# Two orders changed on ScalarE of a one-core transformer layer: four early weight halves, and the transfers that spread the bias rows

## What is computed

```python
# first block
h = rmsnorm(x, norm_mix)
proj = h @ w_in                      # queries, keys, values of two attentions, gates
y_a = swa_sink_attention(...)        # 8 heads, window of 128 keys, bias by distance, one sink
y_b = nsa_attention(...)             # 8 heads: compressed keys, selected blocks, window; bias by distance
merged = sigmoid(g_a) * (y_a @ w_up_a) + sigmoid(g_b) * (y_b @ w_up_b)
x = x + merged @ w_out
ug = causal_dwconv(rmsnorm(x, norm_ffn) @ w_ffn_in, conv_w, conv_b)
x = x + (silu(g) * u) @ w_ffn_out
x = rmsnorm(x, norm_final)
# second block: latent, differential and memory attention, gate, output product
```

## Time and profile before

| what | value |
|---|---|
| median of 3 runs | 1166.47 us (1166.33 to 1166.97) |
| the profiled execution | 1168.41 us, of which the span of the core 1166.6 us |
| PE busy | 1082.8 us, 93% of the span |
| DVE / ACT / POOL busy | 54% / 50% / 33% |
| mean granted clock of PE | 0.962 of full speed |
| DMA | 109.24 MB, mean 94 GB/s |

### The profile page before, as it was taken

How to read it: one execution, slowest core, us unless ns; L and a number is a source line. 1 busy time by engine, 2 the same in 40 slices (tenths; PEclk the granted TensorE clock), 3 DMA queues, 4 the chain that set the end, 5 groups by cost and what they waited for, 6 DMA issues and landing times.

```text
span 1166.6 us, 15532 instructions
## 1 busy us (share of the span) xinstructions
PE 1082.8 (93%) x5162; PEld 894.9 (77%) x5162; DVE 626.5 (54%) x1431; ACT 582.3 (50%) x1176; POOL 389.8 (33%) x172
## 2 busy tenths in 40 slices
PE   6899899799999999999999999999899697888898
PEld 4779688689888787888888888888787576666677
DVE  4535544988835466454554453214255586477631
ACT  5443556888834244444444443324334263778841
POOL 1334544000014444344444444434443243200013
PEclk8989899899999999999999999999899899888999
DMA  5353343101103332223222233323233122341022
GB/s 191 84 165 129 108 138 101 42 19 47 44 34 130 117 101 89 90 94 104 90 99 99 90 107 129 107 90 108 95 130 118 54 91 91 86 113 37 2 72 108
DMA packets 38387, 109.24 MB, mean 94 GB/s; under 512 B 6795, under 2 KB 8971, under 8 KB 37643
## 3 DMA queue, kind: packets, MB, share of 16 engines
q1 hardware_dynamic: 27804, 89.70, 23.5%
q10 hardware_dynamic: 10528, 18.83, 5.1%
HBM read 99.99 MB, written 7.70 MB: 92 GB/s over the span
## 4 chain that ended last, share of the span: by engine, by line
issue 64%; POOL 16%; PE 10%; DVE 5%; ACT 3%; DMA 1%; POOLq 1%; ACTq 0%
POOL WLO L596 16%; PE PS L1680 2%; PE PS L1682 2%; PE PS L1681 2%; ACT PB L789 2%; DVE PB L1227 1%; PE PS L1875 1%; DMA X<-xT 1%; PE PS L1852 1%; DVE PB L1260 1%; POOLq L592 0%; PE PS L2031 0%; DVE PB L1262 0%; ACT HF L764 0%; DVE BLO L1142 0%
## 5 line engine op out<-in xcount | busy, mean ns | idle before, releaser
L596 POOL TENSOR_TENSOR WLO<-RAW,WHI 128x1024 fp32r<-128x1024 f32 x160 | 387.5, 2422 | 765.4 <-ACT WHI L610 765.2
L610 ACT ACTIVATE WHI<-RAW 128x1024 fp32r<-128x1024 f32 x162 | 171.2, 1058 | 318.3 <-PE PS L1682 305.3
L1680 PE MATMUL PS<-HHI,WHI 128*128 128x512 f32 x648 | 259.6, 401 | 28.7 <-POOL WLO L596 19.7
L1681 PE MATMUL PS<-HLO,WHI 128*128 128x512 f32 x648 | 256.7, 396 | 0.0
L1682 PE MATMUL PS<-HHI,WLO 128*128 128x512 f32 x648 | 256.4, 396 | 0.0
L1680 PEld LDWEIGHTS PS<-HHI,WHI 128*128 128x128 f32 x648 | 124.5, 192 | 60.1 <-issue 21.5
L1680 PE MATMUL PS<-BHI,WHI 128*128 128x512 f32 x368 | 146.1, 397 | 2.4 <-DVE BLO L1142 1.3
L1682 PEld LDWEIGHTS PS<-HHI,WLO 128*128 128x128 f32 x648 | 124.3, 192 | 26.5
L1681 PEld LDWEIGHTS PS<-HLO,WHI 128*128 128x128 f32 x648 | 124.3, 192 | 25.9 <-issue 0.5
L1682 PE MATMUL PS<-BHI,WLO 128*128 128x512 f32 x368 | 144.1, 391 | 0.0
L1681 PE MATMUL PS<-BLO,WHI 128*128 128x512 f32 x368 | 144.0, 391 | 0.0
(11 more groups left out here) (286 smaller groups left out, 1652.7 us busy)
## 6 DMA issues: line engine op xcount, KB each, us to landing
RAW<-wstream SPq DMA_DIRECT2D x162, 512.0 KB, 3.3
X<-xT ACTq DMA_DIRECT2D x4, 512.0 KB, 9.5
bias_b<-bias_rows ACTq DMA_DIRECT2D x2, 1024.0 KB
FX<-bias_b ACTq DMA_DIRECT2D x8, 256.0 KB, 2.7
X<-xT ACTq DMA_DIRECT2D x8, 256.0 KB, 3.6
x_keep<-X ACTq DMA_DIRECT2D x2, 1024.0 KB, 4.6
X<-x_keep ACTq DMA_DIRECT2D x2, 1024.0 KB, 5.0
outT<-X ACTq DMA_DIRECT2D x8, 256.0 KB, 2.5
```

What stands on the lines that cost most here:

```text
L596: pool.tensor_tensor(WLO[:, s, :], RAW[:, s, :], WHI[:, s, :].bitcast(F), ALU.subtract).then_inc(split_lo, 1)
L610: act.activation(WHI[:, c % 2, :], RAW[:, c % 2, :], ACT.Copy).then_inc(split_hi, 1)
L1680: pe.matmul(dst, a[0], b[0], start=first, stop=False, **kw)
L1681: pe.matmul(dst, a[0], b[1], start=False, stop=False, **kw)
```

## The change

ACT's list is reordered at four places, and the spreading of the bias rows is cut and moved.

- Projection loop: iteration 0 begins with `stream(4)`; iteration 1 has none; from iteration 2 on each begins with `stream(c + 3)`, one unit further ahead than before. The last one, in iteration 12, is `stream(15)`, so the vtok loop begins at its second unit.
- `stream(19)` moves from behind `blocks_high(1)` to ahead of it.
- `stream(59)` moves from behind the root of the norm to ahead of it.
- `bias_a` goes out in four DMAs of 2 heads (iterations 3 to 6), `bias_b` in four of 2 heads (iterations 7 to 10), `bias_c` in iterations 11 and 12. The wait before the attention is for all 16 DMAs.

```diff
             u = UNIT["proj"]
             for c in range(13):
-                if c >= 2:
-                    stream(u + c + 2)
+                if c != 1:
+                    stream(u + (c + 3 if c else 4))
                 if c < 11:
                     act.wait_ge(scaled, c + 1)
                     ps = PS[:, c % 4, :]
...
                 if c == 3:
                     act.wait_ge(st_rows, 16)
-                    act.dma_start(bias_a, bias_spread(0, 0, 256)).then_inc(spread, 16)
-                if c in (5, 7):
-                    half = (c - 5) // 2 * 4
-                    act.dma_start(bias_b[half:half + 4], bias_spread(8 + half, OH_A, SEQ, 4)).then_inc(spread, 16)
-                if c in (9, 10):
-                    for pg in range(4 * (c - 9), 4 * (c - 9) + 4):
+                if 3 <= c < 7:
+                    h = 2 * (c - 3)
+                    act.dma_start(bias_a[h:h + 2], bias_spread(h, 0, 256, 2)).then_inc(spread, 16)
+                if 7 <= c < 11:
+                    h = 2 * (c - 7)
+                    act.dma_start(bias_b[h:h + 2], bias_spread(8 + h, OH_A, SEQ, 2)).then_inc(spread, 16)
+                if c >= 11:
+                    for pg in range(4 * (c - 11), 4 * (c - 11) + 4):
                         src = bass.AP(tb_dram.tensor, 8 * OH + OH_A + OH_B + 15 * CMP_A + 9 - pg,
                                       [[OH, NH], [-CMP_A, 16], [1, CMP_W]])
                         act.dma_start(bias_c[:, 16 * pg:16 * pg + 16, :], src).then_inc(spread, 16)
...
-            for c in range(4):
+            for c in range(1, 4):
                 if c == 2:
                     blocks_high(0)
                 stream(u + c + 2)
...
             ins.then_inc(v_hi, 1)
+            stream(UNIT["gc"] + 2)
             blocks_high(1)
...
             u = UNIT["gc"]
             for c in range(len(AHEAD)):
-                stream(u + c + 2)
+                if c:
+                    stream(u + c + 2)
                 if c == 0:
-                    act.wait_ge(spread, 16 * 11)
+                    act.wait_ge(spread, 16 * 16)
                     bias_load(0)
                     bias_load(1)
...
             with act.Fori(1, 4) as i:
                 stream_and_norm("wout", 1, 1, x1_done, i)
+            stream(UNIT["ffn"] + 2)
             norm_root(2, RSTD)
...
                     for e in range(2):
                         c = u + 2 * s + e
-                        stream(c + 2, 4, i)
+                        if not isinstance(i, int) or s or e:
+                            stream(c + 2, 4, i)
```

## The result

The kernel became slower: a median of 1173.03 us (1172.98 to 1175.47, 4 runs) beside 1166.40 us of the kernel before on the same chip (1164.72 to 1166.97, 4 runs), a ratio of 1.0072 with a 95% interval of 1.0050 to 1.0094. The forecast was 1164.3 us. The profiled execution took 1175.47 us.

A forecast was written before the change was run, and what follows sets the result against it. PE was taken as the bound, busy 1082.8 of 1166.6 us. Unit 20 later (+0.35), clock recovery (+2.3) and unit 59 (-4.8) sum to -2.15, so 1166.47 became 1164.3 us; range 1158 to 1184.

The forecast's parts named there:

- What bounds the kernel: Whole kernel: PE busy 1082.8 of 1166.6 us, 23.4 us of its waits for `WLO`, with ACT late rather than POOL.
- Unit 4: Projection loop: its high part, no longer behind two evacuations, is ready ahead of PE, saving 3.57 us.
- unit 7: Projection loop: `bias_a` in quarters frees this unit's weight load, saving 3.01 us of stop and 3.0 of slow clock.
- Unit 19: High part ahead of `blocks_high(1)`: saves 2.9 us, or 1.5 with a slow rest, and 2.5 if the clock holds.
- The four terms together, unit 20 at 123.8: Savings of 3.57, 6.0, 2.9 and 2.5 us bring PE to unit 20 at 123.8 instead of 138.76.
- Two heads, two engines, one part after another: Bias transfers: each two-head DMA runs on the same two engines, in turn, at share about 0.13 and 51 GB/s.
- The sum of 83.8 us: Two engines' work on bias rows and weight loads from about 49.4; `spread` complete at 133.2, unit 20 at 139.1.
- This holds whatever the order, since the two engines never run dry: Bias transfers: `spread` completes at 133.2, or 133.5 with its landing, in whatever order the two engines' work comes.
- Unit 59: High part ahead of the norm's root: the 2.88 us stop and 1.9 of slow clock go, -4.8 us.
- ACT's queue takes no more: Rival, chance 0.15: issue blocks at some 175 unmoved rows per engine; unit 20 4.7 us late, about 1169 us.
- The rival of slow 1 KB rows: `bias_a` rows stay slow on two engines: 1196 us at 106 ns a row, 1177 at 70; chance 0.22.
- The rival of other engines: Bias parts find other engines or run side by side, `spread` complete by 118: 1146.8 us; chance 0.10.

The follow-up runs named there:

- proj_only: The kernel before with only the projection loop's and vtok loop's streams one unit further ahead, spreading as before: 1163.82 us, ratio 0.9986.
- spread4_only: The kernel before, its order of high parts kept, with the bias spreading in parts of 4 heads x 64 rows: 1161.95 us, ratio 0.9968.
- u19_only: The kernel before with only unit 19's high part moved ahead of `blocks_high(1)`: 1162.20 us, ratio 0.9970.
- heads4: The changed kernel with each bias part of 4 heads x 64 rows instead of 2 heads x 128 rows: 1146.11 us, ratio 0.9845.
- order_only: The changed kernel with the bias DMAs of the kernel before, the new order of high parts kept: 1153.28 us, ratio 0.9895.
- heads8: The changed kernel with bias parts of 8 heads x 32 rows instead of 2 heads x 128 rows: 1148.56 us, ratio 0.9857.
- spaced2: The spaced run with the short rows issued directly ahead of the wait for `spread` instead of behind unit 18: 1166.17 us, ratio 1.0011.
- ffn_only: The kernel before with only unit 59's high part moved ahead of the root: 1157.36 us, ratio 0.9938.
- narrow_b: The changed kernel with `bias_b` rows of 1 KB instead of 2 KB, second half of each row left out: 1156.62 us, one run.
- spread_only: The kernel before with only the bias DMAs of the changed kernel, its order of high parts kept: 1188.24 us, ratio 1.0200.
- spaced: The changed kernel with two-head `bias_b` parts in iterations 7, 9, 11 and behind unit 16, short rows behind unit 18: 1168.05 us, ratio 1.0029.

## Why the prediction was wrong, step by step

- **What bounds the kernel; that ACT is late and not POOL**: right. Each high part that came early took its stop away.
- **Unit 4, unit 7**: right in the mechanism. Both stops are gone in after, and none of its loads there took longer than 5.9 us, where unit 7's had taken 12.4. In the traces the sizes, 3.6 and 6.0, come out too: the matmul at 83.9 us of before runs at 74.9 in after, 9.0 earlier. In the times of the runs the edits gave less when each was made alone: 1.6 in `proj_only`, 3.7 in `spread4_only`.
- **Unit 19**: right in the stop, 2.21 in after, in `u19_only` and nearly so (2.23) in `heads4`, where 2.3 was said. The 2.5 us of clock beside it came whole in `order_only`, `heads4` and `heads8`, where unit 19 takes 5.6 us (7.97 before), and only in part elsewhere: it takes 7.18 in `u19_only` (128.25 to 135.43) and 7.19 in after.
- **The four terms together, unit 20 at 123.8**: right, once no long hold stood in the way: 122.81 in `heads4`, 126.08 in `heads8`. That `heads4` is nearer owes something to chance, as the two differ already ahead of these edits.
- **Two heads, two engines, one part after another**: right, and the main point of the forecast's argument. Share 0.13 and 51 GB/s, as it said; `bias_a` in by about 80 us, where it said 79. The sum of 83.8 us came out in `spaced2` (133.0). In after the last row had moved by 127.8: while PE stood, fewer loads of weights passed through the two engines, ten where the sum has 14.
- **"This holds whatever the order, since the two engines never run dry"**: this is the step that failed. It is true of the transfers and false of ACT. The sum took an issue as costing ACT some half a microsecond, however many rows lay ahead of it, so it let the high parts of units 13 to 18 go by undisturbed and had only the wait for `spread` stop PE. In after ACT was held in five places for 38.6 us, and PE stopped for 5.63, 4.96, 8.46 and 2.21 us ahead of unit 20, with the clock at a mean of 0.76 between 95 and 153 us where it is 1.00 in `heads4`. That put unit 20 at 152.59, with no wait at `spread` at all; in the forecast it was 139.1, and in `spaced2`, where only one hold stopped PE and the wait for `spread` covered it, 138.49.
- **Unit 59**: right in its mechanism, the stop is gone in after and in `ffn_only`, and is worth 4.6 us in both traces, where 4.8 was said.
- **The rival "ACT's queue takes no more"** was what happened, and had a chance of 0.15. The sign that was named for it, issues of `bias_b` farther apart than the units, is in the trace (9.5 and 11.4 us against 5.4). It was priced low: 1169, with unit 20 at 143.5. Its limit of 175 rows was only the largest number that before had shown, and the one that held the long rows is higher, 210 to 240. But it counted one late issue. Three of `bias_b` were long, then the short rows, which it took for small, held longest (15.77 us), and three of the holds had a stop of their own (5.63, 4.96 and 8.46 us), with slow clock behind. Had the number been 450 or more, nothing would have held ACT and the forecast's sum would have applied; nothing in the trace of before excluded either, which is why both ends of it should have weighed more than 0.15.
- **The rival of slow 1 KB rows** did not occur. **The rival of other engines** was wrong about two heads, but its 1146.8 is what four engines gave: 1146.11.

## What to carry to other kernels

A DMA issue is an instruction in its engine's list: where much is queued, it isn't free, and what stands behind it (here a weight's high part that PE waits for) pays. So count, for each cut of a transfer, how many engines it uses and how many rows that leaves on the fullest one, and cut so that engines stay many: the same bytes in the same number of parts cost 27 us more cut by heads than by rows, most of it by the pace of two engines and the rest by the held issues. And where a change has parts that gain and a part that loses, run them alone; the loss of 0.7% hid a gain of 1% in the order and a loss of 2% in the spreading.

## What the runs showed of the hardware

- **An issue of long rows waits until no more than some 210 to 240 rows are outstanding on an engine's queue.** By the packets of the queue 210 and 224 in after and 235 and 220 in `narrow_b` had not begun to move when an issue ended. In after the issues of `bias_b` end at 73.52, 83.06, 94.46 and 105.87; the last two spacings, 11.4 us, are one part of 128 rows at 80 ns (2 KB at 25.5 GB/s) and one load's 1.28, so ACT was released at the pace of the queue. Whether it is released row by row or in larger steps the traces don't tell: each of these issues ended 1.9 to 3.3 us after the part two before it had moved. The fourth part of `bias_a`, of 1 KB rows, was the first that took longer (1.43, from 64.84), at 222 rows; in `spread_only` the same issue took 0.57, at about the same number. The largest number before was some 170 to 175, with no long issue.
- **The engines of a transfer from DRAM to DRAM are as many as its outermost dimension here**: 8, 4 or 2 heads showed as 0.51 (eight, `heads8` from 86 to 87 us), 0.25 (four) and 0.13 (two) of 16 engines. By the Trainium skill (DMA: Bandwidth & Descriptors, section "Why a DMA increments its semaphore by 16 and not by 1") a DMA issued from ACT uses the largest number of engines up to 16 that divides the slowest dimension of both sides, and the lowest-numbered ones. The traces agree with the number, 0.13 and 51 GB/s for two heads; that one part ran after another agrees with their sharing the same engines, and which engines these are no run here shows.
- **The short rows stay unexplained in their length.** By the count above, four DMAs with 16 rows per engine each should have found room after 64 rows, 5.1 us and a load or two, and took 15.77 (12.22 for seven in `spaced`). The first of the four alone took 9.72, and when it ended only some 130 to 140 rows per engine were outstanding; in `spread4_only` short rows were held at some 90 to 100. So the number above holds for the long rows only, and what the short ones wait for stays open.
- **Executions differ in where slow clock falls**, also where nothing was changed. In `heads4` the clock stood at 0.60 between 20 and 24 us, and in `heads8` at 1.00 there and 0.52 between 31 and 34, ahead of all that the edit touches; it is why the two, 2.4 us apart, are not ranked, and why a difference of under 3 us between two single profiles says little.
